# Second layer of three: the key factors by transposes, one broadcast copy on ScalarE, and a new order of the work of a pair of heads

## The reference, cut to what matters

```python
cq, ckv, k_pe, gate = split(rms_norm_2(x, norm_g) @ w_in)
q  = (rms_norm_2(cq, q_norm_g) @ w_q_up).reshape(b, s, 16, 192)
kv = (rms_norm_2(ckv, kv_norm_g) @ w_kv_up).reshape(b, s, 16, 256)
k  = concatenate([kv[..., :128], broadcast(k_pe)])
q, k = rms_norm_2(q, q_gain), rms_norm_2(k, k_gain)    # over 192 columns, per token and head
o  = softmax(mask(rope(q) @ rope(k).T / sqrt(192))) @ kv[..., 128:]
x  = x + (o * silu(gate)) @ w_out
```

## Time and profile before

| | |
|---|---|
| median of 3 runs | 3364.34 us (3358.56 to 3370.33) |
| the profiled execution, its own time | 3358.49 us |
| its span, first to last instruction | 3356.7 us |
| TensorE busy with products | 3260.4 us, 97% of the span |
| VectorE, ScalarE, GpSimd busy | 1791.8, 1222.6 and 195.6 us |
| mean granted clock of TensorE | 0.993 of full speed |
| the eight pairs of the second layer | from 1764.6 us on, to some 2160 us of the span |

### The profile page before, as it was taken

The page is one execution under the profiler, slowest core; times in us unless marked ns, Lnnn a source line. Parts: engine busy times, 40 slices in busy tenths (PEclk is TensorE's granted clock), DMA queues, the critical chain, the costliest instruction groups (busy, mean ns, idle before and its releaser), DMA issues. The chain is left out here.

```text
span 3356.7 us, 52647 instructions
## 1 busy us (share of the span) xinstructions
PE 3260.4 (97%) x22165; PEld 2666.2 (79%) x22165; DVE 1791.8 (53%) x2970; ACT 1222.6 (36%) x1931; POOL 195.6 (6%) x156
## 2 busy tenths in 40 slices
PE   8999999999999989999999999999999999999999
PEld 6877777777777778867787777887888888888887
DVE  5235555545555546264437777433655566655832
ACT  4123343433333322233225555423334344444421
POOL 1000000000001101100000011010000000000000
PEclk9999999999999999999999999999999999999999
DMA  7423232331122135242342112353322233322452
GB/s 239 112 76 91 86 97 87 94 99 56 53 64 80 47 121 153 76 130 74 94 123 81 35 51 85 110 151 113 88 83 89 81 95 94 95 82 88 159 145 85
DMA packets 492528, 324.30 MB, mean 97 GB/s; under 512 B 27130, under 2 KB 448605, under 8 KB 491782
## 3 DMA queue, kind: packets, MB, share of 16 engines
q1 hardware_dynamic: 492294, 320.94, 32.6%
HBM read 276.05 MB, written 44.85 MB: 96 GB/s over the span
## 5 line engine op out<-in xcount | busy, mean ns | idle before, releaser
L534 PE MATMUL PS<-XH,WHT 128*128 128x512 f32 (+1 forms) x2224 | 898.6, 404 | 7.1 <-DVE AR L1031 2.1
L522 DVE TENSOR_TENSOR WLT<-AR,WHT 128x1024 fp32r<-128x1024 f32 (+1 forms) x430 | 527.6, 1232 | 691.4 <-ACT WHT L516 690.8
L536 PE MATMUL PS<-XH,WLT 128*128 128x512 f32 (+1 forms) x2224 | 871.3, 392 | 0.0
L516 ACT ACTIVATE WHT<-AR 128x1024 fp32r<-128x1024 f32 (+1 forms) x430 | 446.8, 1041 | 652.5 <-PE PS L536 488.8
L535 PE MATMUL PS<-XL,WHT 128*128 128x512 f32 (+1 forms) x1712 | 671.8, 392 | 0.0
L534 PEld LDWEIGHTS PS<-XH,WHT 128*128 128x128 f32 (+1 forms) x2224 | 417.3, 188 | 109.7 <-issue 10.7
L536 PEld LDWEIGHTS PS<-XH,WLT 128*128 128x128 f32 (+1 forms) x2224 | 417.7, 188 | 96.6
L535 PE MATMUL PS<-ARR,WHT 128*128 128x512 f32 x1024 | 404.9, 395 | 0.0
L535 PEld LDWEIGHTS PS<-XL,WHT 128*128 128x128 f32 (+1 forms) x1712 | 321.7, 188 | 70.9 <-issue 4.8
L535 PEld LDWEIGHTS PS<-ARR,WHT 128*128 128x128 f32 x1024 | 192.7, 188 | 40.0 <-issue 0.2
L534 PE MATMUL PS<-XL,WHT 128*128 128x512 f32 x512 | 204.0, 399 | 0.1
(11 more groups left out here) (489 smaller groups left out, 5393.5 us busy)
## 6 DMA issues: line engine op xcount, KB each, us to landing
AR<-b_w_in SPq DMA_DIRECT2D x128, 512.0 KB, 4.0
AR<-w_in SPq DMA_DIRECT2D x122, 512.0 KB, 3.9
AR<-a_w_in SPq DMA_DIRECT2D x48, 512.0 KB, 4.2
AR<-w_out SPq DMA_DIRECT2D x32, 512.0 KB, 4.4
AR<-a_w_out SPq DMA_DIRECT2D x32, 512.0 KB, 4.0
AR<-b_w_out SPq DMA_DIRECT2D x32, 512.0 KB, 4.1
proj_scratch<-AR SPq DMA_DIRECT2D x33, 256.0 KB, 2.2
AR<-a_w_kv_up SPq DMA_DIRECT2D x32, 256.0 KB, 3.4
```

The source lines that it names most:

```text
L516: self.nc.scalar.activation(self.shaped(self.high, n), self.shaped(self.raw, n), ACT.Copy).then_inc(self.s_high, 1)
L522: self.nc.vector.tensor_tensor(self.shaped(self.low, n), self.shaped(self.raw, n), f32(self.shaped(self.high, n)), ALU.subtract).then_inc( ...
L534: mm(out, wh, xh[k0 + c], start=(start and c == 0), stop=False)
L536: last = mm(out, wl, xh[k0 + c], start=False, stop=(stop and c == nk - 1))
```

## The change: what it does

Seven edits, all in the second layer:

1. `key_factors` makes, for each head, four transposes of 128x128 in place of the product of 128x512 with ones. For that SQ[:, e] has to hold the factors themselves, spread along the blocks, and not diagonals.
2. So dg0 on VectorE becomes a copy with a broadcast operand, and dg1 moves to ScalarE as `key_spread`, a copy behind `root` in ScalarE's list, which waits for reck.
3. On TensorE `scores(i, 3)` goes ahead of `key_factors(q, 0)` and `key_factors(q, 1)`.
4. `values(i, 0)` goes ahead of `rotary(q)`; `query(q, 0)` and `swap(q)` go behind `turned(i, 2)`, and `query(q, 1)` behind `turned(i, 3)` and `rotary_sums(q)`.
5. `values(i, 1)`, which stood at the head of the next pair, goes between the two `query_sums`, and `scores(q, 0)` goes behind the last of them, to the end of the pair.
6. On VectorE `scale(i, 2)` goes ahead of `keys(q)`, `bias(i, 3)` and `output(i, 0)` ahead of `rotary_gain(q)`, and the two `split_low` behind them. On ScalarE `rotary_square`, `query_square` and `rotary_high` move between and behind `exps(i, 3)`, `copy(i, 2)` and `copy(i, 3)`.
7. In the part ahead of the loop, `rotary_sums(0)` goes ahead of `query(0, 1)`, and `key_spread(0)` stands behind the root.

```diff
 def key_factors(i, e):
-    N.wait(pe, i, f"dve.dg{e}")
+    N.wait(pe, i, ("dve.dg0", "act.dg1")[e])
     if i:
         V_.wait(pe, i - 1, f"act.{'ab'[e]}")
-    N.did(mm(FB[e][:, :], C("ones"), SQ[:, e, :], start=True, stop=True), "pe", f"rk{e}")
+    for tb in steps:
+        last = nc.tensor.transpose(FB[e][:, blk(tb)], SQ[:, e, blk(tb)], ident)
+    N.did(last, "pe", f"rk{e}")
...
+def key_spread(i):                                          # ScalarE
+    N.wait(act, i, "dve.reck")
+    r = RS[:, TB:2 * TB].unsqueeze(2).broadcast_to([P, TB, P])
+    N.did(A(SQ[:, 1, :].rearrange("p (b t) -> p b t", t=P), r, ACT.Copy), "act", "dg1")
...
-    for e in heads:                                         # VectorE, key_diagonals
+    for e in (0,):
         r = RS[:, e * TB:(e + 1) * TB].unsqueeze(2).broadcast_to([P, TB, P])
-        do(f"dg{e}", TTn(SQ[:, e, :]..., C("ident")..., r, ALU.mult))
+        do(f"dg{e}", V.tensor_copy(SQ[:, e, :].rearrange("p (b t) -> p b t", t=P), r))
...
 root(q, "k")                                                # ScalarE, main loop
+key_spread(q)
 exps(i, 2)
 value_copy(i, 0)
```

More of the change, by code:

```diff
@@ L2376, in latent @@
     N = Marks(k, "mlap",
-              pe=["k0", "k1", "kn", "rk0", "rk1", "qr", "qn0", "qn1", "qrs", "qns"],
-              act=["sk0", "sk1", "rootk", "kh0", "kh1", "krh", "sqr", "sq0", "sq1", "rootq"],
+              pe=["k0", "k1", "kn", "rk0", "rk1", "qr", "qn0", "qrs", "qn1", "qns"],
+              act=["sk0", "sk1", "rootk", "dg1", "kh0", "kh1", "krh", "sqr", "sq0", "sq1", "rootq"],
               pool=["kl0", "kl1", "krl"],
-              dve=["ck0", "ck1", "meank", "reck", "dg0", "dg1", "kg0", "kr0", "kg1", "kr1", "qg", "cqh0", "cq0", "cqh1", "cq1", "meanr", "meanq", "recq", "rq"])
+              dve=["ck0", "ck1", "meank", "reck", "dg0", "kg0", "kr0", "kg1", "kr1", "qg", "cqh0", "cq0", "cqh1", "cq1", "meanr", "meanq", "recq", "rq"])
     W = Marks(k, "mlar", pe=["sw"], dve=["sws", "qc", "qa"], act=["qrh"], pool=["qrl"])
@@ L2670, in _ @@
                           15: [lambda: key_factors(0, 0), lambda: key_factors(0, 1), lambda: rotary(0), lambda: query(0, 0)],
-                          16: [lambda: swap(0), lambda: query(0, 1), lambda: rotary_sums(0)], 17: [lambda: query_sums(0, 0), lambda: query_sums(0, 1)],
+                          16: [lambda: swap(0), lambda: rotary_sums(0), lambda: query(0, 1)], 17: [lambda: query_sums(0, 0), lambda: query_sums(0, 1)],
                           AT - 1: [lambda: scores(0, 0)]})
@@ L2680, in _ @@
                 more = q < NP
-                if i:
-                    values(i - 1, 1)
                 if more:
@@ L2698, in _ @@
                 value(i, 1)
+                scores(i, 3)
                 if more:
@@ L2701, in _ @@
                         key_factors(q, e)
[L2702 to L2706, removed]
                 else:
@@ L2709, in _ @@
                 values(i, 0)
+                if more:
+                    rotary(q)
                 turned(i, 2)
                 if more:
-                    query(q, 1)
+                    query(q, 0)
+                    swap(q)
                 else:
@@ L2717, in _ @@
                     rotary_sums(q)
+                    query(q, 1)
                     query_sums(q, 0)
+                    values(i, 1)
+                    query_sums(q, 1)
                     scores(q, 0)
-                    query_sums(q, 1)
             out_unit(0, 0, 0)
@@ L2839, in _ @@
             after = {6: [lambda: mean_root(0)], 7: [lambda: split_ahead(0)], 10: [rotary_key_square, lambda: mean_root(1)], 11: [lambda: split_ahead(1)],
-                     13: [lambda: key_square(0, 0), lambda: key_square(0, 1), lambda: st.split_high(act, KU[0] + 3)], 14: [lambda: root(0, "k")],
+                     13: [lambda: key_square(0, 0), lambda: key_square(0, 1), lambda: st.split_high(act, KU[0] + 3)], 14: [lambda: root(0, "k"), lambda: key_spread(0)],
                      15: [lambda: st.split_high(act, QRU[0] + 3), lambda: key_high(0, 0), lambda: key_high(0, 1), lambda: rotary_key_high(0), lambda: rotary_square(0), lambda: query_square(0, 0), lambda: st.split_high(act, QNU[0] + 3)],
@@ L2890, in _ @@
                     rotary_key_high(q)
-                    rotary_square(q)
                 exps(i, 3)
                 if more:
-                    query_square(q, 0)
+                    rotary_square(q)
+                copy(i, 2)
                 st.split_high(act, UT + 4 * i + 6)
                 if more:
-                    rotary_high(q)
-                copy(i, 2)
+                    query_square(q, 0)
                 copy(i, 3)
                 if more:
+                    rotary_high(q)
                     query_square(q, 1)
@@ L2964, in key_diagonals @@
                 N.wait(dve, i, "dve.reck")
-                for e in heads:
+                for e in (0,):
                     r = RS[:, e * TB:(e + 1) * TB].unsqueeze(2).broadcast_to([P, TB, P])
-                    do(f"dg{e}", TTn(SQ[:, e, :].rearrange("p (b t) -> p b t", t=P), C("ident").unsqueeze(1).broadcast_to([P, TB, P]), r, ALU.mult))
+                    do(f"dg{e}", V.tensor_copy(SQ[:, e, :].rearrange("p (b t) -> p b t", t=P), r))
             def keys(i):
@@ L3166, in _ @@
                     key_diagonals(q)
+                    scale(i, 2)
                     keys(q)
[L3168 to L3173, removed]
+                    bias(i, 3)
+                    output(i, 0)
                     rotary_gain(q)
-                if more:
+                    scale(i, 3)
+                    st.split_low(dve, UT + 4 * i + 5)
                     query_copy(q, 0)
                     rotary_turn(q)
[L3178 to L3181, removed]
+                    st.split_low(dve, UT + 4 * i + 6)
                     query_copy(q, 1)
@@ L3184, in _ @@
                 else:
+                    st.split_low(dve, UT + 4 * i + 5)
+                    scale(i, 2)
+                    low(i - 1)
+                    bias(i, 3)
+                    output(i, 0)
+                    st.split_low(dve, UT + 4 * i + 6)
                     scale(i, 3)
```

## The result

The changed kernel takes 3375.22 us (median of 20 runs, 3369.82 to 3381.33), the kernel before 3363.56 in the runs beside it (20 runs, 3358.05 to 3372.47). The ratio is 1.0033, with a 95% interval of 1.0026 to 1.0039: slower by 11.1 us by the ratio, 11.7 by the two medians. The forecast was 3368 in a range of 3351 to 3380; the time lies inside it, 7 us above the forecast, at the place of the slower rival (3374.7).

The account below looks back on a forecast made before the run. TensorE, 97% busy, bounds the kernel. Pairs stay at 49.64 us; -1.5 at the last pair and +5.1 for three clock falls give +3.6: 3362.1 against the profiled 3358.49, 3368 on the median, range 3351 to 3380.

Parts of the forecast that it names:

- the slower rival: Clock falls in every pair: 7 x 1.7 - 1.5 = +10.4 us, 3374.7; chance 0.14.
- The work of a pair: TensorE's pair of heads, second layer: 12.89 + 16.21 + 20.54 = 49.64 us, the same as before.
- The two new waits: TensorE waits ahead of scores(i, 2), about 1.5 us, and around the key factors' transposes, 2.3 us.
- the 49.64 of the sum: Forecast length of a pair without clock falls, in us, unchanged from the kernel before.
- The side sum: TensorE's work between the starts of scores(0, 0) and scores(0, 2) in pair 0: some 11.4 us.
- the largest gain: scores(i, 3) ahead of the key factors: its gain taken by the copy behind the root, exponentials 3.30 us later.
- I count three: Clock falls in the seven pairs: three assumed, 5.1 us; bounds none and seven, 11.9 us.
- The price of 1.7: Loss per clock fall: 3.5 us at 0.52 of full speed, 3.5 x 0.48 = 1.7 us.
- -1.5: Without falls, scores(7, 2) in the last pair start at 2124.18 against 2125.66, 1.5 us earlier.
- the two earlier stands: TensorE in the profile before: a thin 3.0 us stretch with a clock fall, a 2.6 us stand without.
- Ahead of the loop the same 0.88 us is worth nothing: Start of the layer: transposes save 0.88 us, but TensorE stands 2.6 us for the rotary key anyway.
- The faster rival: Copy does not hold the exponentials: load ahead of it, 3353.7; no ScalarE delay reaching TensorE, 3346.7; chance 0.17.

Follow-up runs that it names:

- experiment 2: Changed kernel plus nine unused products in the waits around the key factors' transposes; 3364.78 us, ratio 0.9997 to the kernel before.
- experiment 1: Changed kernel with the second broadcast copy back on VectorE behind the first; 3346.36 us, ratio 0.9944 to the kernel before.
- experiment 7: Changed kernel with ScalarE's broadcast copy moved behind the exponentials of block 2; 3349.94 us, ratio 0.9959 to the kernel before.
- experiment 3: Changed kernel with values(i, 1) back at the next pair's head and scores(q, 0) between the query sums; 3369.33 us, ratio 1.0018 to the kernel before.
- eighth experiment: Changed kernel, copy on VectorE, values at old place, rotary sums behind second query, ten unused products at layer start; 3339.97 us, ratio 0.9938 to the kernel before.
- experiment 6: Changed kernel's new order, with key factors as products and both diagonals on VectorE; 3353.37 us, ratio 0.9970 to the kernel before.
- experiment 5: Kernel before with key factors as transposes, both copies on VectorE, old order; 3360.48 us, ratio 0.9989 to the kernel before.

## Why the prediction came out as it did

**The work of a pair** was right. The two new waits came where they were put and at their length: 12.96 against 12.89 for the third scores, 15.86 against 15.81 for the transposes, and without falls (experiment 2) a pair of 49.64, which is the 49.64 of the sum. (The side sum of TensorE's work ahead of the third scores, "some 11.4", adds up to 11.3; nothing hangs on it.) That the largest gain is eaten by the copy behind the root is shown by experiments 1 and 7: with the copy on VectorE or behind the exponentials the same change is faster by 0.4 to 0.6%.

**The step that was mis-sized** is the count in "So a fall is possible in each of seven pairs, and certain in none; I count three". The price of 1.7 was right, the count is seven in this profile. From the first scores of pair 0 to the third of pair 7 the profile before has 361.08 us and the one after 371.39 (1772.71 to 2144.10): 10.3 more, where -1.5 + 7 x 1.7 gives 10.4. This is the slower rival as it was written, which I had at 0.14 beside 0.62 for fewer falls. The time lies in the range only because that was drawn wide enough for the rival; for the number of falls I had no argument. I had set the two earlier stands against each other, one with a fall and one without, and taken the middle; but all seven pairs repeat the same stretch at the same length, so that they need not be seven independent cases. That is argued, not shown; experiment 3, with the same stretch in pairs of another length, had five of seven, and what spared its other two stays open.

**"Ahead of the loop the same 0.88 us is worth nothing"** was right in that nothing is won, and left the clock out. TensorE stands there in both kernels, for 2.58 us before and for 4.14 after, until the rotary key comes; ScalarE's split ahead of it waits for a load of weights, and starts 0.35 ahead of the first key factors (1649.26) before, 0.36 behind them (1654.16) after. First the two rows of before, then those of after:

```profile
1648.91 1.06 ACT L516 ACTIVATE WHT<-AR 128x1024 fp32r<-128x1024 f32 x1 [8.42 <-DMA AR<-a_w_in]
1653.73 0.50 PE L564 MATMUL PS<-RESR,WHT 128*128 128x512 f32 x1 [2.58 <-DVE AR L2975]
...
1654.52 1.06 ACT L516 ACTIVATE WHT<-AR 128x1024 fp32r<-128x1024 f32 x1 [8.23 <-DMA AR<-a_w_in]
1659.34 0.79 PE L564 MATMUL PS<-RESR,WHT 128*128 128x512 f32 x1 [4.14 <-DVE AR L2982]
```

So the 0.88 us saved comes back as wait, and 0.7 more with the later load. The windows of the profile after:

```profile
1656.00:1660.00 4.00, 0.66 (x2) 0.57 (x3) 3.97 (x7) 2.80 (x4) 0.00 (x0) 0.76 0.38 102
1660.00:1663.00 3.00, 3.00 (x9) 2.32 (x8) 2.58 (x2) 1.31 (x3) 2.76 (x2) 0.50 0.42 126
```

A fall of some 6 us lies there, which the profile before doesn't have the earlier trace rows; from the first key factors to the first scores it took 115.32 us before (1649.26 to 1764.58) and 118.55 after (1654.16 to 1772.71), 3.2 more: the 0.7 of the load, and some 2.5 of the clock. All profiles but those of the kernel before and of the eighth experiment show a fall at this place, a short or a long one, that with products in place of transposes (experiment 6) among them, so the transposes aren't its only cause. One profile each can't say how often the kernel before falls there, nor whether the later load is more than chance.

**The sum of the profiles.** Pairs 10.3, start of the layer 3.2, all that lies ahead of the key factors of pair 0 4.9 (they begin at 1649.26 and 1654.16) and all behind the third scores of pair 7 -1.5 make the 16.9 between the spans. The last two lie almost wholly in code that wasn't changed; the medians of 20 runs, 11.1 us apart by the ratio, are the better measure, and they lie between the pairs alone and the pairs with the start.

**The faster rival** is out in the form it had: the load does not run ahead of the copy. Its other price, 3346.7 if nothing of ScalarE's delay reached TensorE, is what the change takes with the copy on VectorE (experiment 1, 3346.36).

**The rules of the skill.** By the page on TensorE (The Trainium skill, TensorE: Matmul & The Clock Gate, part 4) transposes don't count as work for the clock like products. The seven falls fit it but don't test it: in experiment 2 the added products take the place of standing still and not of the transposes, and in experiment 5 the same eight transposes within 2.7 us bring no fall, so the rule alone doesn't tell the two cases apart. Whether two products in those same 3.1 us would have held the clock wasn't tried. The drain of 1.38 us behind a table load (The Trainium skill, ScalarE: Activation LUTs, What ACT_TABLE_LOAD costs) isn't there: the load runs from 1847.33 for 1.28 us, and the exponential starts at 1848.63, 0.02 behind it.

## What to carry to other kernels

An instruction that is moved to a half empty engine costs what it waits for, not what it lasts: a copy of 0.6 us held the exponentials up by 3.3, and with them TensorE by 2.3 (49.64 against 47.34 a pair), because it stood ahead of the chain's next link, waited for another engine's later result, and pushed a table load out of its cover. When a change puts all of TensorE's waits of a period into one place, price the clock with it: a loop repeats the same thin stretch in each turn, so falls in nearly every turn are a case of their own with a full price (seven of seven here, five of seven in experiment 3), not the far end of an average. And try each part of a change alone; here the order alone was worth 0.3%, the transposes alone 0.1%, which can't be told from nothing, both together 0.6%, and one misplaced copy turned them into a loss.

## What the runs showed of the hardware

A stretch of 3.1 us with eight transposes of 0.1 us each was followed by a fall of the granted clock to its lower level in all seven pairs of the changed kernel and in five of seven in experiment 3; one of 2.7 us with the same eight was followed by none in seven pairs. Each fall cost 1.7 us. Nine rounded products of 0.23 us without use, put into the waits, brought these 1.7 us back in every pair, at no cost. ScalarE's table load lasted 1.28 us, with the exponential 0.02 behind it, and its copy with a broadcast operand 0.61 to 0.63, behind the root as well as behind the exponentials (experiment 7) without a load of its own. The code ahead of the pairs put the first key factors at 1649.26 to 1660.27 us in the profiles, with falls of the clock at varying places of the first layer, so that one profile alone can't carry a difference of some us in the sum, while the length of the pairs 1 to 6 repeats within 0.3 us where each has the same number of falls.
